# A decay-gated attention block on one core: the next softmax exponential ahead of the decay's, decay levels on halves, scores copied under masks

## What is computed

```
bcum = cumsum(log_a)                                   # per channel, along the tokens
decay[i, j] = exp(bcum[i] - bcum[j])   for j <= i
A[i, j] = sum_d q[i, d] * k[j, d] * decay[i, j, d]
o_intra = A @ v
```

## Time and profile before

| | |
|---|---|
| median of 3 runs (range) | 2305.14 us (2303.09 to 2305.76) |
| profiled execution, its span | 2306.5 us; no other time of that execution is given |
| PE, DVE, ACT, POOL busy | 98%, 75%, 56%, 19% of the span |
| chain that ended last | PE 88%, DVE 6%, ACT 3%, DMA 2% |
| second attention's 16 items | 1270.62 to 1388.91 us, 118.3 us or 5% of the span |
| PE busy in it | 109.45 us of 118.29, at a mean granted clock of 0.91 |

### The profile page before, as it was taken

The page is one execution under the profiler, slowest core; times in us unless marked ns, Lnnn a source line. Parts: engine busy times, 40 slices in busy tenths (PEclk is TensorE's granted clock), DMA queues, the critical chain, the costliest instruction groups (busy, mean ns, idle before and its releaser), DMA issues.

```text
span 2306.5 us, 47728 instructions
## 1 busy us (share of the span) xinstructions
PE 2259.2 (98%) x15260; PEld 2044.9 (89%) x15260; DVE 1726.9 (75%) x3749; ACT 1298.3 (56%) x2725; POOL 440.5 (19%) x264
## 2 busy tenths in 40 slices
PE   9999999999999999999999999999999999999999
PEld 3888899999999888888978678999999999888887
DVE  4687768888788777776657775768888888777776
ACT  3476555555587555555547234565555587555554
POOL 0000000776671000000000000000767682000000
PEclk9999999999999999999999899999999999999999
DMA  8777445777755666665455224545776755666665
GB/s 321 255 242 240 159 156 181 184 183 181 183 129 159 206 210 209 207 212 182 162 175 163 70 73 130 196 159 182 182 183 182 182 129 154 211 206 210 208 209 168
DMA packets 191116, 422.84 MB, mean 183 GB/s; under 512 B 54288, under 2 KB 88336, under 8 KB 190624
## 3 DMA queue, kind: packets, MB, share of 16 engines
q1 hardware_dynamic: 150112, 413.73, 54.6%
q0 software_dynamic: 36864, 0.15, 4.3%
q10 hardware_dynamic: 4032, 7.64, 0.9%
HBM read 403.48 MB, written 17.96 MB: 183 GB/s over the span
## 4 chain that ended last, share of the span: by engine, by line
PE 88%; DVE 6%; ACT 3%; DMA 2%; issue 1%; SPq 0%; POOL 0%; DVEq 0%; ACTq 0%; POOLq 0%
PE ps L1988 21%; PE ps L897 14%; PE ps L899 14%; PE ps L898 14%; PE ps L1989 10%; PE ps L922 9%; PE ps L2297 2%; DMA ring<-stream 2%; PE ps L1643 1%; PE ps L1621 1%; PE ps L2020 1%; ACT arena L658 1%; DVE hl L2067 0%; PE ps L1054 0%; DVE ring_lo L593 0%
## 5 line engine op out<-in xcount | busy, mean ns | idle before, releaser
L1988 PE MATMUL ps<-csplit,hl 128*128 128x512 f32 x2048 | 724.0, 399 | 4.5 <-issue 3.5
L2221 POOL DMA_INDIRECT gates<-gbuf,picks_at x256 | 439.1, 1715 | 1446.6 <-issue 1010.0
L897 PE MATMUL ps<-hsplit,hl 128*128 128x256 f32 x2048 | 583.4, 285 | 0.0
L899 PE MATMUL ps<-hsplit,hl 128*128 128x256 f32 x2048 | 580.4, 283 | 0.0
L898 PE MATMUL ps<-hsplit,hl 128*128 128x256 f32 x2048 | 580.3, 283 | 0.0
L1989 PE MATMUL ps<-csplit,hl 128*128 128x256 f32 x2048 | 575.9, 281 | 0.0
L2064 ACT CAST hl<-ring 128x512 fp32r<-128x512 f32 x562 | 342.7, 619 | 299.2 <-PE ps L899 294.0
L2067 DVE TENSOR_TENSOR hl<-ring,hl 128x512 fp32r<-128x512 f32 x562 | 385.9, 693 | 125.3 <-ACT hl L2064 105.7
L1988 PEld LDWEIGHTS ps<-csplit,hl 128*128 128x128 f32 x2048 | 385.5, 188 | 100.6 <-issue 5.4
L2404 DVE TENSOR_TENSOR hl<-ring,hl 128x512 fp32r<-128x512 f32 x508 | 351.3, 692 | 76.8 <-ACT hl L2394 64.1
L898 PEld LDWEIGHTS ps<-hsplit,hl 128*128 128x128 f32 x2048 | 393.7, 192 | 0.0
(11 more groups left out here) (376 smaller groups left out, 3137.4 us busy)
## 6 DMA issues: line engine op xcount, KB each, us to landing
ring<-stream SPq DMA_DIRECT2D x675, 512.0 KB
s_area<-stream SPq DMA_DIRECT2D x48, 512.0 KB, 5.1
gates<-zeros SPq DMA_DIRECT2D x32, 512.0 KB, 5.0
gring<-gates SPq DMA_DIRECT2D x256, 64.0 KB, 3.1
gates<-gbuf,picks_at POOLq DMA_INDIRECT x256
arena<-xc ACTq DMA_DIRECT2D x2, 1024.0 KB, 15.5
arena<-keys ACTq DMA_DIRECT2D x2, 1024.0 KB, 9.1
gbuf<-consts ACTq DMA_DIRECT2D x1, 1120.0 KB, 5.2
```

Source lines behind the costliest of these rows:

```text
L897: pe.matmul(out_ap, w[0], m[0], start=start, stop=False)
L899: return pe.matmul(out_ap, w[0], m[1], start=False, stop=stop)
L1988: pe.matmul(ps[:, bank, :], w_hi, m_both, start=start, stop=False)
L2221: pool.indirect_dma_start(out=cells, out_offset=bass.IndirectOffsetOnAxis(ap=picks_at[:, i, c:c + 1], axis=0), in_=gates[:, i, c:c + 1], i ...
```

## The change

It has four parts. Line numbers of the changed kernel are its own; L1904 becomes L1930, L1704 becomes L1710, and so on.

1. ACT does the softmax exponential of item i+1 right after item i's tile, ahead of the copies of the transposed probabilities and of the decay's exponential.
2. `pieces_early` deals the fill with rounding up: items 3, 7, 11 and 15 have no tile.
3. The decay levels work on halves: the distance subtracts for left and right runs with the right sign (so the operation that made it positive is gone, and the exponential's scale too), q is faded in the right runs only and k in the left ones. Level 7 uses q and k as they are.
4. The scores are copied from PSUM into `amat` under the mask, in the right runs only, which needs `amat` at zero: POOL does two memsets after `qn_ready`.

```
+    def pieces_early(group, parts):
+        n = [m for g in group for m in g]
+        at = [-(-len(n) * i // parts) for i in range(parts + 1)]
+        return [n[a:b] for a, b in zip(at, at[1:])]
...
         def act(self, eng):
+            for i in range(self.ahead):
+                self.act_exponential(eng, i)
             for i, it in enumerate(self.items):
                 m = self.i0 + i
...
+                if not self.ahead:
+                    self.act_exponential(eng, i)
                 take_tiles("act", eng, self.fill[i])
+                if self.ahead and i + self.ahead < len(self.items):
+                    self.act_exponential(eng, i + self.ahead)
                 eng.wait_ge(S("att_turned"), m + 1)
...
     def dve_gla_distance(dve, m):
...
-            for h in range(GLA_HEADS):
-                bh = lb[:, h, a:a + P].rearrange("p (m s) -> p m s", s=2 * size)
-                dh = gd[:, h, :].rearrange("p (m s) -> p m s", s=2 * size)
-                r = bh[:, :, size - 1:size].broadcast_to([P, P // (2 * size), 2 * size])
-                ins = dve.tensor_tensor(dh, bh, r, ALU.subtract)
-            chain(ins, dve)
-            dve.scalar_tensor_tensor(gd, gd, -1.0, gd, ALU.mult, ALU.max).then_inc(S("gla_dist"), 1)
+        edge = left(n, b)[:, :, :, size - 1:size].broadcast_to([P, GLA_HEADS, P // (2 * size), size])
+        dve.tensor_tensor(left(n, gd), edge, left(n, b), ALU.subtract)
+        dve.tensor_tensor(right(n, gd), right(n, b), edge, ALU.subtract).then_inc(S("gla_dist"), 1)
...
     def dve_gla_fade(dve, m):
...
-            dve.tensor_tensor(gqd[m % 2], gd, gq[:, :, a:a + P], ALU.mult)
-            ins = dve.tensor_tensor(gkd[m % 2], gd, gk[:, :, a:a + P], ALU.mult)
+        dve.tensor_tensor(right(n, gqd[m % 2]), right(n, gd), right(n, gq[:, :, a:a + P]), ALU.mult)
+        dve.tensor_tensor(left(n, gkd[m % 2]), left(n, gd), left(n, gk[:, :, a:a + P]), ALU.mult)\
+           .then_inc(S("gla_faded"), 1)
...
     def collect(dve, m):
...
-        ins = dve.tensor_tensor(atmp, src, mask, ALU.mult)
-        chain(ins, dve)
-        dve.tensor_tensor(amat[t], amat[t], atmp, ALU.add).then_inc(S("gla_kept"), 1)
+        if n == LEVELS:
+            ins = dve.copy_predicated(amat[t], mask, src)
+        else:
+            ins = dve.copy_predicated(right(n, amat[t]), right(n, mask), right(n, src))
+        ins.then_inc(S("gla_kept"), 1)
...
     def pe_gla_level(pe, m):
...
-        pe.wait_ge(S("gla_faded"), m + 1)
+        pe.wait_ge(S("gla_faded"), fades_to(m))
...
+            k, q = (gkd[m % 2][:, h, :], gqd[m % 2][:, h, :]) if n < LEVELS else (gk[:, h, a:a + P], gq[:, h, a:a + P])
...
+                if b == 2:
+                    pool.wait_ge(S("qn_ready"), 1)
+                    for t in range(NT):
+                        ins = pool.memset(amat[t], 0.0)
+                    ins.then_inc(S("amat_zeroed"), 1)
```

More of the change, by code:

```diff
@@ L465, in build @@
     gd2, gqd, gkd, amat = [gd2_0, gd2_1], [gqd_0, gqd_1], [gkd_0, gkd_1], [amat_0, amat_1]
-    qdec, kdec_0, kdec_1, atmp, blast = over("cq", (GLA_HEADS, T), (GLA_HEADS, META), (GLA_HEADS, P), (GLA_HEADS, P),
-                                             (2, GLA_HEADS))
+    qdec, kdec_0, kdec_1, blast = over("cq", (GLA_HEADS, T), (GLA_HEADS, META), (GLA_HEADS, P), (2, GLA_HEADS))
     kdec = [kdec_0, kdec_1]
@@ L1592, in build, with __init__ @@
     class Attention:
-        def __init__(self, items, n_keys, key_tiles, scale, probs, pt, fill, ready, outs, step=None, parts=None):
+        def __init__(self, items, n_keys, key_tiles, scale, probs, pt, fill, ready, outs, step=None, parts=None, ahead=0):
+            self.ahead = ahead
             self.step = step
@@ L1694, in dve_part, with act_exponential @@
             eng.tensor_tensor(lo[:, x, :], raw[:, x, :], hi[:, x, :].bitcast(F32), ALU.subtract).then_inc(S("attn2_split"), 1)
+        def act_exponential(self, eng, i):
+            it, m = self.items[i], self.i0 + i
+            b = (m % 2) * 8
+            p = self.probs[:, m % 2, 0:self.n_keys]
+            eng.wait_ge(S("att_max"), m + 1)
+            if it["sink"] is not None:
+                eng.activation(small[:, b + 3:b + 4], v_("sink", it["sink"]), ACT.Exp, bias=small[:, b + 1:b + 2])
+            eng.activation(p, p, ACT.Exp, bias=small[:, b + 1:b + 2],
+                           accum_out=small[:, b + 2:b + 3]).then_inc(S("att_exp"), 1)
         def act(self, eng):
+            for i in range(self.ahead):
+                self.act_exponential(eng, i)
             for i, it in enumerate(self.items):
                 m = self.i0 + i
[L1699 to L1705, removed]
+                if not self.ahead:
+                    self.act_exponential(eng, i)
                 take_tiles("act", eng, self.fill[i])
+                if self.ahead and i + self.ahead < len(self.items):
+                    self.act_exponential(eng, i + self.ahead)
                 eng.wait_ge(S("att_turned"), m + 1)
@@ L1848, in dve_gla_level, with sides, left, right @@
             dve_gla_distance(dve, m + 1)
+    def sides(n, ap):
+        return ap.rearrange("p h (m two s) -> p h m two s", two=2, s=1 << n)
+    def left(n, ap):
+        return sides(n, ap)[:, :, :, 0, :]
+    def right(n, ap):
+        return sides(n, ap)[:, :, :, 1, :]
     def dve_gla_distance(dve, m):
@@ L1853, in dve_gla_distance, with fades_to @@
         a = t * P
-        gd = gd2[(t * LEVELS + n) % 2]
-        if n < LEVELS:
-            size = 1 << n
-            for h in range(GLA_HEADS):
-                bh = lb[:, h, a:a + P].rearrange("p (m s) -> p m s", s=2 * size)
-                dh = gd[:, h, :].rearrange("p (m s) -> p m s", s=2 * size)
-                r = bh[:, :, size - 1:size].broadcast_to([P, P // (2 * size), 2 * size])
-                ins = dve.tensor_tensor(dh, bh, r, ALU.subtract)
-            chain(ins, dve)
-            dve.scalar_tensor_tensor(gd, gd, -1.0, gd, ALU.mult, ALU.max).then_inc(S("gla_dist"), 1)
+        if n == LEVELS:
+            return
+        gd, b = gd2[(t * LEVELS + n) % 2], lb[:, :, a:a + P]
+        size = 1 << n
+        edge = left(n, b)[:, :, :, size - 1:size].broadcast_to([P, GLA_HEADS, P // (2 * size), size])
+        dve.tensor_tensor(left(n, gd), edge, left(n, b), ALU.subtract)
+        dve.tensor_tensor(right(n, gd), right(n, b), edge, ALU.subtract).then_inc(S("gla_dist"), 1)
+    def fades_to(m):
+        return sum(n < LEVELS for _, n in gla_steps[:m + 1])
     def dve_gla_fade(dve, m):
@@ L1903, in act_gla_level @@
             gd = gd2[dist % 2]
-            act.activation(gd, gd, ACT.Exp, scale=-1.0).then_inc(S("gla_fade"), 1)
+            act.activation(gd, gd, ACT.Exp).then_inc(S("gla_fade"), 1)
     def pe_gla_level(pe, m):
@@ L1908, in pe_gla_level @@
             return
-        pe.wait_ge(S("gla_faded"), m + 1)
+        t, n = gla_steps[m]
+        a = t * P
+        pe.wait_ge(S("gla_faded"), fades_to(m))
         wait(pe, "gla_kept", m)
         for h in range(GLA_HEADS):
-            mm = pe.matmul(ps[:, GLA_BANK, h * P:(h + 1) * P], gkd[m % 2][:, h, :], gqd[m % 2][:, h, :],
-                           start=True, stop=True)
+            k, q = (gkd[m % 2][:, h, :], gqd[m % 2][:, h, :]) if n < LEVELS else (gk[:, h, a:a + P], gq[:, h, a:a + P])
+            mm = pe.matmul(ps[:, GLA_BANK, h * P:(h + 1) * P], k, q, start=True, stop=True)
         mm.then_inc(S("gla_pair"), 1)
```

21 lines of the change are left out of this document (8 added, 13 removed).

## The result

The changed kernel takes 2282.0 us (median of 4 runs, 2276.48 to 2291.85) against 2304.11 us (4 runs, 2299.11 to 2305.76). The ratio is 0.9915, with a 95% interval of 0.9887 to 0.9942: 19.6 us less by the ratio, between 13.4 and 26.0. The forecast was 8.7 us less, the range ended at 14.1. It was faster, as forecast, and by more than twice as much.

A forecast was written before the change was run, and what follows sets the result against it. The prediction took PE, busy 98% of the span, as the bound. Its terms, 7.6 + 3.4 - 1.7 - 0.6 = 8.7 us less, gave a median of 2296.4 us, with a range of 2291 to 2301.

The forecast's parts named there:

- what bounds the items: Second attention: PE's own work per item is the floor, 7.04 us with a tile and 3.58 us without.
- which waits go: Second attention: PE's waits for normalised probabilities (5.2 us) and kept decay scores (2.4 us) go, 7.6 us gained.
- the second slow stretch: The 6.8 us at 1.2 GHz from 1362.80 lose their cause, a 2.6 us wait; 3.4 us gained.
- The first stretch at 1.2 GHz stands as it is: The 13.5 us from 1270.62 stay, since the 2.15 us idle before them end with the unchanged rotary embedding on DVE.
- costs nothing: Dealing a tile to item 0 puts it into the first slow stretch, with as many microseconds spent there as before.
- Rival A: First slow stretch of the second attention ends after 6.8 us, another 3.4 us gained, 2293.0 us; chance 0.21.
- The term of -1.7 us: Ten items with a tile: ACT's exponential ahead of the probability copies delays PE's value sums by 0.17 us each.
- The term of -0.6 for item 14: Item 14, with no scores behind its transposes: the value sums begin at 1.70 us instead of 1.10.
- B: Waits in items 14 and 15 make the clock fall anew; 3.4 to 6.8 us lost, 2299.8 to 2303.2 us; chance 0.13.
- C: The exponential on ACT is not really ahead, tileless items still wait; 0.1 us gained, 2305 us; chance 0.07.
- D: DVE's new decay instructions become the bound and the kernel slower; 19 us more, 2324 us; chance 0.03.

The follow-up runs named there:

- e3: The kernel before with only the next item's softmax exponential moved ahead on ACT, old fill and decay levels; ratio 0.9955 to the kernel before.
- e4: The kernel before with only the decay levels on halves, masked copies and POOL's memsets, old fill and exponential order; ratio 0.9958 to the kernel before.
- e5: The kernel before with only the early fill (`pieces_early`); ratio 0.9974 to the kernel before.
- e6: The kernel before with the exponential ahead and the early fill, decay levels as before; ratio 0.9917 to the kernel before.
- e7: The changed kernel without the exponential ahead, so levels on halves and early fill; ratio 0.9927 to the kernel before.
- e8: The changed kernel with the old fill, so levels on halves and exponential ahead; ratio 0.9945 to the kernel before.
- e12: The changed kernel with item 0's tile behind its transposes instead of ahead of them; ratio 0.9935 to the kernel before.
- e10: The kernel before, unchanged, profiled a third time; ratio 1.0001, span 2305.4 us.
- e11: The changed kernel, unedited, profiled a third time; ratio 0.9935 to the kernel before, span 2291.4 us.
- e1: The kernel before, unchanged, profiled a second time; ratio 1.0004.

## Why the prediction was wrong, point by point

**Right: what bounds the items, and which waits go.** PE's own work was the floor: items of 7.05 and 3.59 us were measured for 7.04 and 3.58. The 7.6 us of waits went; at full clock S fell by 7.3 (means of three profiles each, 113.6 and 106.4).

**Right: the second slow stretch.** It went with its wait, 3.4 us.

**Wrong: "The first stretch at 1.2 GHz stands as it is", and that the tile in item 0 "costs nothing".** This is the step that failed. The stretch shrank from 13.65 us to 3.4 to 10.2, which is worth 1.7 to 5.1 us. Rival A had the mechanism, with a chance of 0.21 and with 6.8 us as its only length. The experiments bear it out: it follows the fill and not the other parts (e3 to e8), and it needs the tile, not the missing wait (e12). My slip was to ask only what began the stretch, the 2.15 us of idle time, and not what ended it: in the kernel before, the clock rose at 1284.26, 1.9 us after the first tile began (1282.38), and the change brings that tile forward. The kernel before, ahead of that tile, in its first 1.88 us and behind them:

```profile
1270.62:1282.38 11.76, 11.53 (x29) 6.71 (x30) 8.28 (x26) 2.89 (x8) 0.00 (x0) 0.50 0.00 0
1282.38:1284.26 1.88, 1.88 (x6) 1.52 (x6) 1.88 (x5) 0.00 (x0) 0.00 (x0) 0.50 0.00 0
1284.26:1290.00 5.74, 5.74 (x31) 4.41 (x30) 1.20 (x4) 1.88 (x6) 0.00 (x0) 1.00 0.34 70
```

The rule of the Trainium skill that I set beside rival A (TensorE: Matmul & The Clock Gate, section "What's actually happening"), that the lower clock is the default state and activity releases it, was the better guide to the direction. The runs agree with it, with one thing to add: PE was busy for 11.53 of the 11.76 us ahead of that tile, and the clock stayed at 0.50 all the same.

**Mis-sized: what the change adds.** The term of -1.7 us for ten items measured 0. I had let the copies wait for the whole accumulator read; they start 0.09 us after it begins, and the sums begin 1.54 us after the transposes as they did before (1.53). The term of -0.6 for item 14 measured -0.44.

With these the sum is 7.6 + 3.4 + (1.7 to 5.1) - 0.4 = 12.3 to 15.7, against 12.4 to 16.0 measured in S (15.7 between e10 and e11).

**Not foreseen: the expert loops.** The forecast took it for granted that unchanged code takes unchanged time. The rest of the 22 us between the first medians and of the 31.8 between the first profiles lies there, and 11.6 of the 31.8 in the two expert loops. A step of an expert loop takes 2.77 or 2.83 us, for the whole loop, and a loop has 128 products with the gates, about 7 us. In e5 the two loops of one execution differ. DVE's product with the gates, two steps of the first loop and two of the second (start us, us, instruction):

```profile
881.53 0.28 DVE L2344 TENSOR_TENSOR arena<-arena,gring 128x128 f32 x1
...
884.30 0.28 DVE L2344 TENSOR_TENSOR arena<-arena,gring 128x128 f32 x1
...
2086.80 0.28 DVE L2344 TENSOR_TENSOR arena<-arena,gring 128x128 f32 x1
...
2089.64 0.28 DVE L2344 TENSOR_TENSOR arena<-arena,gring 128x128 f32 x1
```

That is 2.77 and 2.84. PE waits in neither loop: over 260 us of each (800 to 1060 and 2000 to 2260) it is busy for 260.00 us at a clock of 1.00, so the products themselves follow each other a little more slowly. All runs together, the kernel before took 2292 to 2315 us (103 runs, mean 2304.0) and the changed one 2276 to 2296 (19 runs, mean 2286.9). That is a wider spread than the range given, which took the first three runs' 2.7 us for the noise. Loop 1 was at 2.77 in five of the eight profiles with the early fill and in none of the six with the old one; it runs long before the second attention, with the same instructions. Against a tie to the fill speaks that the kernel before also ran in 2292.17 us at a mean granted clock of 0.993, the clock of its profiled 2306.20 us (e1): 14 us less without a better clock is what two faster loops would give. That run has no trace, so it is not shown, and what sets the step stays open. The 17.0 us between the two means may thus hold a part that is not the change's; what the traces show for it is the 12.4 to 16.0 us in S.

**The rivals that didn't come.** B: the waits at the end were 1.05 and 0.6 us, and the clock held there in all profiles of the changed kernel. The mechanism exists all the same: in e5 the clock fell behind 0.86 and 0.94 us of waits, shorter than the 2.15 us that the prediction took for the shortest that does it. C: the exponential is far enough ahead; a tileless item waits for nothing. D: five decay instructions take 2.1 to 2.4 us, and DVE idles.

## What to carry to other kernels

Where two engines hand work to each other in a circle, first look at the order on the engine that serves both: moving one instruction ahead of another took 7.4 of 7.6 us of waits here, a lighter DVE 4.6 of them, and the two gains don't add. Price a stretch at the low clock as something that the work inside it can shorten, and the idle time before it as something to fill: one tile there took 4.0 to 7.2 us off S. Compare two profiles place by place, so that a gain in unchanged code isn't booked to the change. And take the spread between executions from more than three of them before writing a range narrower than it.

## What the runs showed of the hardware

A copy under a mask from PSUM to SBUF, 256 elements a partition, takes 0.43 to 0.44 us, and 0.73 us where the runs are one or two elements long; 512 in one run take 0.74. Products with the same short runs, SBUF to SBUF, stay at 0.42. ACT's copy behind an activation with an accumulator read starts 0.09 us after that read begins. After an idle time of 2.15 us the clock fell in all 13 profiles that had it and stayed down for 3.4 to 13.65 us; it rose 1.9 to 5.3 us after the first tile began. It fell for 3.4 us behind two waits of 0.86 and 0.94 us in one profile (e5), and held behind 1.50 and 0.93 us in another (the kernel before). And a PE-bound loop of fixed instructions can run its steps at 2.77 or at 2.83 us from its start to its end, at a granted clock of 1.00 in both.
